# Hybrid S5, convolution and MoE block: the first four projection tiles take rows without the norm's scale

## What is computed

```python
h = concatenate([meta, x])                    # 272 x 1024
y = h * rsqrt(mean(h * h) + 1e-6)             # one scale per row
z = (y * norm_mix_g) @ w_in                   # 1024 -> 3584 columns
u, conv_in, gate_a, gate_b = split(z)         # 512, 1024, 1024, 1024
ya = gelu(s5_scan(u));  ya = (ya @ w_s5_lin) * sigmoid(ya @ w_s5_gate)
yb = silu(layernorm(causal_conv31(val * sigmoid(gate)))) @ w_conv_out
h = h + (sigmoid(gate_a) * ya + sigmoid(gate_b) * yb) @ w_out
h = h + top4_of_32_experts(rmsnorm(h))        # clamped SwiGLU, float32 weights
out = rmsnorm(h)[16:]
```

## Time and profile before

| | |
|---|---|
| median of 3 runs | 1207.38 us (1207.24 to 1212.56) |
| profiled execution | 1206.97 us |
| its span | 1205.0 us, mean granted clock 0.994 |
| PE busy | 1131.6 us, 94% |
| DVE busy | 321.5 us, 27% |
| ACT busy | 188.2 us, 16% |
| POOL busy | 44.6 us, 4% |
| DMA | 436.43 MB, mean 362 GB/s |

### The profile page before, as it was taken

One profiled execution on the slowest core, in us unless ns is written; L12 is line 12 of the kernel. 1 busy time (PEld: TensorE's weight loads), 2 busy tenths in 40 slices (PEclk: granted clock), 3 DMA queues, 4 the chain that ended last, 5 costly groups with the idle time before them and its releaser, 6 DMA issues.

```text
span 1205.0 us, 17752 instructions
## 1 busy us (share of the span) xinstructions
PE 1131.6 (94%) x7148; PEld 533.9 (44%) x7149; DVE 321.5 (27%) x756; ACT 188.2 (16%) x279; POOL 44.6 (4%) x45
## 2 busy tenths in 40 slices
PE   6999999999999999988999998888888899999995
PEld 5877887543333433333334333333333333433332
DVE  7899253631111211111112111111111112211112
ACT  1311230411111111111111111111111111111002
POOL 1002050300000000000000000000000000000000
PEclk9999999899999999999999999999999999999998
DMA  9562594493999999998899999999999889999994
GB/s 266 176 167 88 171 416 194 153 408 143 392 429 431 428 427 429 431 428 367 357 429 429 431 426 428 429 431 426 427 429 431 357 367 431 428 427 429 429 429 176
DMA packets 57399, 436.43 MB, mean 362 GB/s; under 512 B 11056, under 2 KB 27504, under 8 KB 32704
## 3 DMA queue, kind: packets, MB, share of 16 engines
q1 hardware_dynamic: 57248, 436.03, 87.6%
q10 hardware_dynamic: 128, 0.08, 0.0%
HBM read 432.72 MB, written 1.05 MB: 360 GB/s over the span
## 4 chain that ended last, share of the span: by engine, by line
PE 66%; DMA 27%; DVE 3%; ACT 1%; issue 1%; ACTq 0%; SPq 0%; DVEq 0%
PE ps L1449 29%; DMA ring<-in_w_gate_up 27%; PE ps L1460 13%; PE ps L1215 7%; PE ps L1432 4%; PE ps L1351 2%; PE ps L1398 2%; PE ps L1423 2%; PE ps L1301 1%; PE ps L1363 1%; PE ps L1482 1%; ACT rD L722 1%; PE ps L1469 1%; PE ps L1415 1%; DMA ring<-in_ssm_a_im 0%
## 5 line engine op out<-in xcount | busy, mean ns | idle before, releaser
L1449 PE MATMUL ps<-ring,rD 128*64 128x512 f32 x1664 | 368.1, 594 | 32.1 <-DMA ring<-in_w_gate_up 31.6
L1460 PE MATMUL ps<-ring,rD 128*64 128x512 f32 x1120 | 248.0, 595 | 16.0 <-ACT rD L722 15.9
L1449 PEld LDWEIGHTS ps<-ring,rD 128*64 128x64 f32 x1664 | 119.7, 137 | 266.2 <-issue 210.0
L1460 PEld LDWEIGHTS ps<-ring,rD 128*64 128x64 f32 x1120 | 79.8, 137 | 157.6 <-issue 157.4
L1149 DVE TENSOR_SCALAR rD<-ps 128x512 f32<-128x512 f32 x35 | 24.2, 692 | 424.4 <-PE ps L1449 424.4
L1215 PE MATMUL ps<-ring 128*128 128x256 f32 (+1 forms) x448 | 103.6, 391 | 1.7 <-DVE ring L829 1.7
L720 ACT ACTIVATE rD<-rD 128x512 f32<-128x512 f32 x35 | 22.0, 629 | 493.6 <-DVE rD L1149 493.6
L1215 PEld LDWEIGHTS ps<-ring 128*128 128x128 f32 x448 | 85.4, 193 | 17.6 <-issue 3.4
L1075 DVE CAST rE<-rE 128x64 bf16 (+1 forms) x36 | 7.0, 196 | 298.0 <-PE ps L1449 297.7
L1432 PE MATMUL ps<-rD,rE 64*128 64x512 f32 x288 | 71.5, 615 | 0.7 <-ACT rD L726 0.7
L1423 PEld LDWEIGHTS ps<-rE,rC 128*128 128x128 bf16 x1728 | 57.2, 98 | 27.3 <-issue 26.9
(11 more groups left out here) (328 smaller groups left out, 701.5 us busy)
## 6 DMA issues: line engine op xcount, KB each, us to landing
ring<-in_w_gate_up SPq DMA_DIRECT2D x96, 2048.0 KB, 20.3
ring<-in_w_down SPq DMA_DIRECT2D x64, 2048.0 KB, 24.5
late<-in_w_gate_up SPq DMA_DIRECT2D x16, 2048.0 KB, 24.4
early<-in_w_gate_up SPq DMA_DIRECT2D x16, 2048.0 KB, 28.7
ring<-in_w_in SPq DMA_DIRECT2D x14, 1024.0 KB, 6.5
ring<-in_w_out SPq DMA_DIRECT2D x4, 1024.0 KB, 17.1
ring<-late SPq DMA_DIRECT2D x16, 142.0 KB, 3.2
ring<-in_w_s_lin SPq DMA_DIRECT2D x2, 1024.0 KB, 5.7
```

Source lines behind the costliest of these rows:

```text
L1449: ins = nc.tensor.matmul(ps[64 * h:64 * h + 64, a, :], xT[:, k, :], gsl[odd][n][:, at:at + 512], start=False, stop=(k == KT - 1), skip_gro ...
L1460: ins = nc.tensor.matmul(ps[64 * h:64 * h + 64, 2, :], actT[:, k % 4, 64 * (k // 4):64 * (k // 4) + 64], dsl[odd][k // 4][:, at:at + 512], ...
```

## The change

Tiles z0 to z3 multiply w_in with `hraw`, the transposed rows times g but without the row's scale. The scale is put on their result `uT` by one product on DVE. Tiles z4 to z27 use `hT` = `hraw` times `rbc` as before. Around this:

- `norm_mix_g` is loaded by ACT's queue, second behind the meta rows, and no more by SP. PE transposes g first, then the meta rows, block 0, block 1; `h_tr` is raised for each column group of block 1. DVE copies g before its meta squares.
- On DVE the norm's chain stands in front of the time-step exponential, and the eight `hraw` steps in front of both.
- The scale broadcast (`row_scales`) stands behind z1 and uses banks 4 and 5, the transposes of the discretised rows (`discretised`) behind z3, `parameters` and ACT's `sine_tables` behind z5.
- In the table `between`, `bc` moves from before z8 to before z11, and the later entries back by up to four tiles. POOL's fill of `bq` also waits for the eight `hT` steps, the scan's first input for the scaled u.

```diff
         hT = view(rB, 0, KT, L)
+        hraw = view(rD, 0, KT, L)
-        between = {8: [("bc", 0)], 9: [("in", 0), ("k", 0)], 10: [("in", 1)], 14: [("out", 0)], 16: [("conv", 0), ("in", 2)],
+        between = {11: [("bc", 0)], 12: [("in", 0), ("k", 0)], 13: [("in", 1)], 18: [("out", 0)], 19: [("conv", 0), ("in", 2)],
...
@@ SP
-            sp.dma_start(rows1[0:8, :], T["norm_mix_g"].rearrange("o (m p) -> (o m) p", p=P)).then_inc(gmix_in, 16)
@@ POOL
-            pool.wait_ge(h_tr, 1)
+            pool.wait_ge(h_tr, KT)
             pool.wait_ge(sumsq, 1)
             pool.wait_ge(disc_rows, 1)
+            pool.wait_ge(h_scaled, KT)
             nc.gpsimd.memset(bq, 0.0).then_inc(bq_zero, 1)
@@ ACT
             act.dma_start(xin[0:META, 2, :], T["meta_tokens"]).then_inc(x_in[2], 16)
+            act.dma_start(rows1[0:8, :], T["norm_mix_g"].rearrange("o (m p) -> (o m) p", p=P)).then_inc(gmix_in, 16)
...
-                    if m == 3:
+                    if m == 5:
                         sine_tables()
@@ DVE
+            dve.wait_ge(gmix_tr, 1)
+            nc.vector.tensor_copy(colp[:, 0:8], ps[:, 7, L:L + 8]).then_inc(gmix_cols, 1)
+            dve.wait_ge(gmix_cols, 1)
             dve.wait_ge(x_in[2], 16)
             link(nc.vector.tensor_tensor(metasq, xin[0:META, 2, :], xin[0:META, 2, :], ALU.mult))
             link(nc.vector.tensor_reduce(ss[0:META, 2:3], metasq, AX_X, ALU.add))
-            dve.wait_ge(par_in, 16 * 3)
-            exp(dts, ldt, 2, NB)
...
+            for k in range(KT):
+                dve.wait_ge(h_tr, k + 1)
+                nc.vector.tensor_scalar(hraw[:, k, :], ps[:, k, 0:L], colp[:, k:k + 1], None, ALU.mult).then_inc(h_raw, 1)
...
-            dve.wait_ge(gmix_tr, 1)
-            link(nc.vector.tensor_copy(colp[:, 0:8], ps[:, 7, L:L + 8]))
+            dve.wait_ge(par_in, 16 * 3)
+            exp(dts, ldt, 2, NB)
...
+            dve.wait_ge(h_raw, KT)
             for k in range(KT):
-                nc.vector.scalar_tensor_tensor(hT[:, k, :], ps[:, k, 0:L], colp[:, k:k + 1], rbc, ALU.mult, ALU.mult
-                                               ).then_inc(h_dve, 1)
+                nc.vector.tensor_tensor(hT[:, k, :], hraw[:, k, :], rbc, ALU.mult).then_inc(h_scaled, 1)
...
             nc.vector.engine_nop().then_inc(phases, 1)
+            dve.wait_ge(mm_act, 4)
+            u = uT.rearrange("p m t n -> p m n t")
+            nc.vector.tensor_tensor(u, u, rbc.rearrange("p (n t) -> p n t", t=2).unsqueeze(1).to_broadcast([P, MT, NCK, 2]),
+                                    ALU.mult).then_inc(u_scaled, 1)
@@ PE
-            for c, rows, at in ((0, P, META), (1, P, META + P), (2, META, 0)):
+            pe.wait_ge(gmix_in, 16)
+            nc.tensor.transpose(ps[:, 7, L:L + 8], rows1[0:8, :], ident[0:8, 0:8]).then_inc(gmix_tr, 1)
+            for c, rows, at in ((2, META, 0), (0, P, META), (1, P, META + P)):
...
+                    if c == 1:
+                        ins.then_inc(h_tr, 1)
...
+                h = hraw if z < 4 else hT
                 for k in range(KT):
                     if z == 0:
-                        pe.wait_ge(h_dve, max(k + 1, 2))
+                        pe.wait_ge(h_raw, k + 1)
+                    if z == 4:
+                        pe.wait_ge(h_scaled, k + 1)
...
-                    pe.wait_ge(mm_act, 4)
+                    pe.wait_ge(u_scaled, 1)
...
                     z_tile(n)
+                    if n == 1:
+                        row_scales()
                     if n == 3:
+                        discretised()
+                    if n == 5:
                         parameters()
```

More of the change, by code:

```diff
@@ L249, in build @@
         sumsq, ms_ready, root, rbc_mm = sem("sumsq"), sem("ms_ready"), sem("root"), sem("rbc_mm")
[L250 removed]
+        h_tr, h_raw, gmix_in, gmix_tr = sem("h_tr"), sem("h_raw"), sem("gmix_in"), sem("gmix_tr")
+        h_scaled, u_scaled, gmix_cols = sem("h_scaled"), sem("u_scaled"), sem("gmix_cols")
         par_tr, par_cols, disc_rows = sem("par_tr"), sem("par_cols"), sem("disc_rows")
@@ L299, in build @@
         PE_ORDER = []
-        between = {8: [("bc", 0)], 9: [("in", 0), ("k", 0)], 10: [("in", 1)], 14: [("out", 0)], 16: [("conv", 0), ("in", 2)],
-                   17: [("conv", 1)], 18: [("out", 1), ("in", 3), ("conv", 2)], 20: [("conv", 3), ("out", 2)],
-                   22: [("mean", 0)], 23: [("out", 3)], 25: [("gelu", 0)]}
+        between = {11: [("bc", 0)], 12: [("in", 0), ("k", 0)], 13: [("in", 1)], 18: [("out", 0)], 19: [("conv", 0), ("in", 2)],
+                   20: [("conv", 1)], 21: [("out", 1), ("in", 3), ("conv", 2)], 23: [("conv", 3), ("out", 2)],
+                   24: [("mean", 0)], 25: [("out", 3)], 26: [("gelu", 0)]}
         for z in range(2 * N_IN):
@@ L1184, in _, with row_scales, discretised @@
             pe.wait_ge(consts, 7)
-            for c, rows, at in ((0, P, META), (1, P, META + P), (2, META, 0)):
+            pe.wait_ge(gmix_in, 16)
+            nc.tensor.transpose(ps[:, 7, L:L + 8], rows1[0:8, :], ident[0:8, 0:8]).then_inc(gmix_tr, 1)
+            for c, rows, at in ((2, META, 0), (0, P, META), (1, P, META + P)):
                 pe.wait_ge(x_in[c], 16)
                 for k in range(KT):
+                    if c == 2 and k == KT - 1:
+                        pe.wait_ge(gmix_cols, 1)
                     ins = nc.tensor.transpose(ps[:, k, at:at + rows], xin[0:rows, c, k * P:(k + 1) * P],
                                               ident[0:rows, 0:rows])
-            ins.then_inc(h_tr, 1)
-            pe.wait_ge(gmix_in, 16)
-            nc.tensor.transpose(ps[:, 7, L:L + 8], rows1[0:8, :], ident[0:8, 0:8]).then_inc(gmix_tr, 1)
-            pe.wait_ge(disc_rows, 1)
-            for c in range(4):
-                ins = nc.tensor.transpose(ps[:, 6, L + NB * c:L + NB * c + NB], arow[:, c, :], ident[0:NB, 0:NB])
-            ins.then_inc(disc_tr, 1)
-            pe.wait_ge(scales, 3)
-            for c, rows, b, at in ((2, META, 0, 0), (0, P, 0, META), (1, P, 1, 0)):
-                ins = nc.tensor.matmul(ps[:, b, L + at:L + at + rows], ones[0:rows, :], diag[0:rows, c, 0:rows],
-                                       start=True, stop=True)
-            ins.then_inc(rbc_mm, 1)
+                    if c == 1:
+                        ins.then_inc(h_tr, 1)
+            def row_scales():
+                pe.wait_ge(scales, 3)
+                for c, rows, b, at in ((2, META, 4, 0), (0, P, 4, META), (1, P, 5, 0)):
+                    ins = nc.tensor.matmul(ps[:, b, L + at:L + at + rows], ones[0:rows, :], diag[0:rows, c, 0:rows],
+                                           start=True, stop=True)
+                ins.then_inc(rbc_mm, 1)
+            def discretised():
+                pe.wait_ge(disc_rows, 1)
+                for c in range(4):
+                    ins = nc.tensor.transpose(ps[:, 6, L + NB * c:L + NB * c + NB], arow[:, c, :], ident[0:NB, 0:NB])
+                ins.then_inc(disc_tr, 1)
             def z_tile(z):
```

18 lines of the change are left out of this document (8 added, 10 removed).

## The result

The changed kernel takes 1201.41 us, median of 5 runs (1199.63 to 1201.85), against 1207.87 us (5 runs, 1207.24 to 1212.56): ratio 0.9939, 95% interval 0.9924 to 0.9954. Forecast were 1199.0 us and a range of 1196.6 to 1202.2, so the range holds, in its upper part. The median lies above the forecast's own core of 1198 to 1200, among the times that R1 had (1200 to 1202.2). The profiled execution took 1199.63 us around a span of 1197.6 us and is the fastest of the five; against the profiled one of before (1206.97) it is 7.3 us shorter, where the medians differ by 6.5.

What follows compares the result with a forecast made beforehand. PE was taken to bound the kernel until about 240 us, then expert weight DMA at a fixed rate. Terms -8.2 + 0.9 - 1.1 = -8.4 us gave 1198.6 profiled, median 1199.0 us; range 1196.6 to 1202.2.

Steps and rivals of the forecast that it cites:

- R1: Rival: late start from late g or slot 0, or a longer slow stretch, up to 3.2 us: 1200 to 1202.2; chance 0.15.
- The start of z0: First projection tile: starts at 9.6 us instead of 17.78, 8.2 us earlier; bounds 9.2 and 12.0.
- (a): Condition for z0: g columns land at 5.6 us through ACT's queue; DVE finishes the meta rows at 8.6.
- (b): Condition for z0: PE transposes from 5.9, first column of block 1 at 8.9, raw column 0 ready for 9.4.
- (c): Condition for z0: weight slot 0 lands at 9.3 to 9.6 us, against 9.64 before.
- The start-up loss: Tiles z0 to z3 at PE's slow rate: loss kept at 1.8 us, bounds 0 and 3.6.
- PE's own additions: Broadcast matmuls after z1, 0.6 us, and transposes of discretised rows after z3, 0.3 us: PE cost 0.9 us.
- The meetings: Where PE meets the discretisation chain: slack 0.2 us at z8 and 0.4 us at the B and C transposes.
- R2: Rival: the wait changes place because slacks at z8 and the B and C transposes are small: 1200.5 to 1204; chance 0.12.
- the 1.1 us of that term: PE's gap before output 0 disappears: gain 1.1 us.
- The sum on PE: Terms -8.2 + 0.9 - 1.1 give -8.4 us on PE.
- Everything moves with it: Behind 157.67 us, from the variance to the kernel's end, everything moves with PE's gain of 8.4 us.

Runs made afterwards that it cites:

- warm start: Changed kernel plus six idle products before PE's first wait, the u product's axes reordered, and idle products in the router's last two waits: 1199.07 us, ratio 0.9932.
- old table: Changed kernel with the table `between` of the kernel before, so B and C transposes before z8 and output 0 before z14: 1213.77 us, ratio 1.0052.
- kernel before with idle products: Kernel before plus three idle 512-column matmuls ahead of the expert choice's product in the router: 1209.40 us, ratio 1.0011.
- product on u in the other order: Changed kernel with the product scaling u written with u contiguous on its innermost axis and the scale read at stride two: 1200.19 us, ratio 0.9943.
- product on u twice: Changed kernel with a second, unused DVE product of 1088 columns in front of the u scaling: 1200.57 us, ratio 0.9941.
- three groups: Kernel before plus idle products in three router waits: before the logits, the expert choice's product and the rank's product: 1207.91 us, ratio 1.000.
- Filling both waits: Changed kernel plus three idle 512-column products before the expert choice and four of 128 columns ahead of the rank's product: 1198.42 us, ratio 0.9925.

## Why the prediction was right, and where it was not

**The start of z0: right value, one term left out.** Forecast 9.6, measured 9.79, by conditions (a), (b) and (c). g's transpose began at 5.29 for 5.6, the raw columns at 8.61 for the 8.6 of (a). But the sum compared slot 0 and raw column 0 and took the transposes of block 1 only up to their first column. PE issues all eight before z0 and is through with them at 9.8. The warm start showed that this is what binds (z0 moved with the transposes), and the run with the old table too: transposes 0.33 us shorter, z0 0.28 earlier. With all eight in, the prediction's own figures (from 5.9 on, 0.8 and 3.6 us of transposes) give 10.3; the transposes began at 5.38 instead of 5.9, which brought z0 back to the forecast. That is luck. Slot 0, issued at 1.72 and landing in 7.7 us at 9.42, would have allowed 0.4 us less.

**The start-up loss: assumed at 1.8, measured 0.8 and 0.7.** z0 and z1 took 8.26 us by the chain, 7.45 at the full rate, and z2 and z3 were at full rate. The step that failed is that transposes "don't count as PE being busy; the trace agrees". In the trace of before all transposes are indeed slow, the wide ones at 421 ns and the narrow ones at 262 to the last. But that is one execution. In the kernel before with idle products, which has the same instructions up to there, the narrow ones fell to 209 ns by 9.4 us and the weight loads from 219 to 138; in the runs with the old table and with the product on u in the other order the last wide ones of block 1 were fast as well, with weight loads down to 140 ns for 230. The Trainium skill, TensorE: Matmul & The Clock Gate, section Part 4: PE-mode transpose, says that they don't count as activity; by these runs they do. The loss then isn't a fixed term. Nine profiles have the change's raw tiles behind its transposes, and z0 and z1 took by the chain 8.26, 8.11, 8.45 and 8.50 us, 7.62 behind the warm start, and 7.45 to 7.48 in the other four: from nothing to 1.0 us. That the transposes are why z0 and z1 lose less than the 1.8 is argued from it, not shown by itself.

**PE's own additions: 0.9 forecast.** From start to start the broadcast held PE for 0.87 us (18.18 to 19.05) for the 0.6 of the step, the discretised rows for 0.35 (26.48 to 26.83) for 0.3. z0 to z3 gave 0.58 us back: 16.40 us before, 8.39 and 7.43 after. In all, PE took 0.72 us more between z0 and the product behind the variance than before, its gap of 1.16 us left out.

**The meetings.** At z8 PE didn't wait. The last sine ended at 39.83, the table load took 1.28 us, and the activation began at its end, 41.15. By the Trainium skill, ScalarE: Activation LUTs, section What ACT_TABLE_LOAD costs, 1.38 us of drain come on top of such a load; this trace disagrees, with 1.32 us from one activation to the next, load included. At the B and C transposes PE arrived without a visible gap, but with next to nothing to spare (forecast 0.4): DVE's last step (L912) ended at 52.98 and the transposes began at 53.13, the same 0.15 us behind it as in the run with the product on u twice, where PE did wait; there, 1.96 us more on DVE became a wait of 1.88. The product on u took 2.10 us for the 1.3 of the sum, because its innermost axis isn't contiguous. That alone would have used up the slack; the rest of DVE's chain was 0.3 us shorter than in the sum and PE 0.3 us later, so that R2 stayed away by luck. At output 0 the gap of 1.16 us went, and with the old table it was there again to the hundredth: the 1.1 us of that term are shown. That the table has to be moved back at all is shown by the same run, 10.94 us of waiting.

**The sum on PE, 8.4 us, came out at 8.43.** The terms were 8.2 + 1.1 - 0.9, measured 7.99 + 1.16 - 0.72. That they agree to the hundredth is luck: the start-up alone moves this figure by up to a microsecond from one execution to the next, and the same product came between 148.10 and 149.68 in profiles that differ from the change only behind it or in the order of the product on u.

**From there to the end: the step that failed.** "Everything moves with it" held for the stretch from the first gate-up product on, but not for the router. What failed is that the sum left "the slow-clock stretch around 236" as it is. The stretch's place relative to PE's waits changed: before, it was 6.8 us long and lay on a product that the wait for the masks covered, and had cost 0.16 us (shown by the three groups in the kernel before); after, it was 3.4 us long and lay on the gather, where it cost 1.17 us, and 1.0 us of the gain went. R1 had it as "a longer slow stretch"; it was shorter, but uncovered. Filling both waits brought the gather back to 1.57 us. The median fell from 1201.41 and 1200.32 to 1198.42, which is more than the gather explains; of the 1.4 us between the profiled executions, 0.97 are the router and 0.53 the start-up, less 0.1 behind the first gate-up product.

**From the profile to the median.** The forecast for the profiled execution was 1198.6 us and it took 1199.63: the missing microsecond is the router's. The median was then set 0.4 us above it, as in the kernel before; it came 1.8 above. These 1.4 us are the larger part of the distance between 1199.0 and 1201.41, and no term of the prediction held them.

What stays open is where the other executions of after lose them. The three that took longest (1201.41 to 1201.85 us) have a mean granted clock of 0.992, the other two 0.995 and 0.996. Over 1198 us, 0.003 to 0.004 is an estimated 7 to 10 us more at the 1.2 GHz level, so the clock is the likely cause. But the router and the start-up both change between executions, and the record doesn't tell them apart. The kernels with the router's waits filled, at 0.996 to 0.998, spread over 0.9, 1.4 and, with the warm start, 1.8 us, against 2.2, which speaks for the router as a part of it.

## What to carry to other kernels

A scale per row that follows the input can be put on the product's result; the gain is what the scale's chain had held back, but only if the other work of that chain is made due later too. Here the same edit with the old order of parts was 0.5% slower. When two kernels differ by a shift in time, look at what each PE clock drop covers or uncovers: a product at the lower clock that ends before its successor's input is there costs next to nothing (0.16 us here for a stretch of 6.8), and a shorter stretch on a product that others wait for costs in full (1.17 us). A range should hold that as a term. And a single profile isn't enough to take a start-up loss or a slack from: here the loss went from nothing to 1.0 us with the same instructions.

## What the runs showed of the hardware that was not expected

- Transposes alone raised PE's rate. With nothing else on PE ahead of them, the narrow ones went from 262 to 209 ns by 9.4 us and their weight loads from 219 to 138 ns (kernel before with three idle products); with the old table the weight loads of the wide ones went from 230 to 141 ns. In other executions of the same instructions they stayed slow to the end. The granted-clock column prints 1.00 from the start, so only durations show the lower rate there.
- Three idle products of 512 columns in a wait of 3.03 us didn't keep the clock up for the gather; with four of 128 columns in the 1.09 us behind as well it stayed up (2.74 to 1.57 us), and in all four profiles with both groups the granted clock is 1.00 from 200 to 250 us. The stretch also moves by itself: without any idle product in the router the gather took 1.57 us in two profiles of variants of the changed kernel, with the stretch on the residual.
- Idle products ahead of the first transposes (2.93 us of them) didn't make the transposes faster: 4.61 us with and without.
- A product of 1088 columns on DVE with the short axis innermost takes 2.10 us, 1.29 with the long one innermost.
- A table load on ACT between activations of two sets took 1.28 us, and from the end of the one to the start of the other it was 1.32 us.
